# Gated linear attention: products of constants on TensorE at four kinds of waits

## What is computed

```python
def _gla_chunked(q, k, v, logg, s0):            # chunks of c = 64 tokens, 4 heads, dk = 32, dv = 64
    b = jnp.cumsum(logg.reshape(bsz, n, c, h, dk), axis=2)
    b_last = b[:, :, -1:]
    qe = q * jnp.exp(b)
    ke = k * jnp.exp(-b)
    att = jnp.where(causal, jnp.einsum('bnihd,bnjhd->bnhij', qe, ke), 0.0)
    o_intra = jnp.einsum('bnhij,bnjhv->bnihv', att, v)
    u = jnp.einsum('bnjhd,bnjhv->bnhdv', k * jnp.exp(b_last - b), v)
    decay = jnp.exp(b_last[:, :, 0])
    def step(state, xs):
        dec, uc = xs
        return dec[..., None] * state + uc, state
    s_fin, s_prev = lax.scan(step, s0, (decay by chunk, u by chunk))
    o_inter = jnp.einsum('bnihd,nbhdv->bnihv', qe, s_prev)
    return o_intra + o_inter, s_fin

def _gla_mixer(gq, gk, gv, glow, gr, s0, w_gate, b_gate, norm_g):
    logg = log_sigmoid(glow @ w_gate + b_gate) / 16
    o, s_fin = _gla_chunked(q / sqrt(32), k, v, logg, s0)
    return rmsnorm(o, norm_g) * silu(gr), s_fin
```

## Time and profile before

| | |
|---|---|
| median of 3 runs | 3492.03 us |
| the profiled execution's own time | 3492.51 us |
| its span, first to last instruction | 3490.8 us |
| PE busy | 3169.1 us, 91% of the span |
| DVE busy | 1812.2 us, 52% |
| ACT busy | 909.2 us, 26% |
| mean granted PE clock | 0.937 of full speed |

### The profile page before, as it was taken

How to read it: one execution, slowest core, us unless ns; L and a number is a source line. 1 busy time by engine, 2 the same in 40 slices (tenths; PEclk the granted TensorE clock), 3 DMA queues, 4 the chain that set the end, 5 groups by cost and what they waited for, 6 DMA issues and landing times. The chain is left out here.

```text
span 3490.8 us, 50998 instructions
## 1 busy us (share of the span) xinstructions
PE 3169.1 (91%) x20834; PEld 2795.9 (80%) x20834; DVE 1812.2 (52%) x3100; ACT 909.2 (26%) x1461; POOL 244.5 (7%) x280
## 2 busy tenths in 40 slices
PE   5986899799989999999979588998988999999998
PEld 5963477555889999999979455765568999999998
DVE  3853477444345454454556545774442554545445
ACT  3013344344231111111220224443442311111112
POOL 2000000242000000000020000003400000000000
PEclk9985799899999999999989758998999999999999
DMA  4111101364121111111021201015621211111111
GB/s 96 43 36 32 38 5 37 121 196 134 49 57 49 49 47 36 54 54 37 21 45 38 54 10 35 5 37 184 208 95 27 61 55 36 49 50 45 36 43 66
DMA packets 226512, 207.04 MB, mean 59 GB/s; under 512 B 50244, under 2 KB 195780, under 8 KB 226132
## 3 DMA queue, kind: packets, MB, share of 16 engines
q1 hardware_dynamic: 200728, 119.38, 12.7%
q0 software_dynamic: 25600, 85.11, 8.0%
HBM read 193.58 MB, written 11.05 MB: 59 GB/s over the span
## 5 line engine op out<-in xcount | busy, mean ns | idle before, releaser
L189 PE MATMUL ps<-streamH,upH 128*128 128x344 f32 x2112 | 449.9, 321 | 3.4 <-DVE upL L2291 3.4
L189 PE MATMUL ps<-streamH,upL 128*128 128x344 f32 x2112 | 448.4, 321 | 0.0
L189 PE MATMUL ps<-streamL,upH 128*128 128x344 f32 x2112 | 447.2, 320 | 0.0
L189 PEld LDWEIGHTS ps<-streamH,upH 128*128 128x128 f32 x2112 | 356.0, 188 | 4.1 <-DVE upL L2291 3.7
L189 PEld LDWEIGHTS ps<-streamH,upL 128*128 128x128 f32 x2112 | 357.0, 189 | 0.0
L189 PEld LDWEIGHTS ps<-streamL,upH 128*128 128x128 f32 x2112 | 353.9, 188 | 0.0
L2229 ACT ACTIVATE upH<-hc 128x1024 fp32r<-128x1024 f32 x88 | 93.5, 1063 | 975.4 <-PE ps L189 972.9
L2351 DVE TENSOR_TENSOR xT<-xT,ps 128x1032 f32<-128x1032 f32 x176 | 216.1, 1229 | 227.5 <-PE ps L189 227.5
L415 PE MATMUL ps<-inH,inW 128*128 128x344 f32 (+1 forms) x1248 | 237.4, 326 | 41.4 <-DVE inW L467 41.4
L2312 DVE TENSOR_TENSOR hc<-ps,rstd 128x1032 f32<-128x1032 f32 x44 | 54.3, 1233 | 371.4 <-PE ps L189 371.4
L415 PEld LDWEIGHTS ps<-inH,inW 128*128 128x128 f32 (+1 forms) x1248 | 201.4, 185 | 49.0 <-DVE inW L467 42.8
(11 more groups left out here) (461 smaller groups left out, 5093.0 us busy)
## 6 DMA issues: line engine op xcount, KB each, us to landing
hc<-in_w_ffn_in SPq DMA_DIRECT2D x88, 512.0 KB, 3.8
hc<-in_w_ffn_out SPq DMA_DIRECT2D x44, 512.0 KB, 3.7
big<-in_w_in SPq DMA_DIRECT2D x22, 512.0 KB, 3.9
stream_raw<-in_w_out SPq DMA_DIRECT2D x16, 512.0 KB, 4.0
big<-in_x_prompt SPq DMA_DIRECT2D x1, 4096.0 KB
out_y_prompt<-big SPq DMA_DIRECT2D x8, 512.0 KB
scratch_y<-hc SPq DMA_DIRECT2D x16, 136.0 KB
scratch_u<-wring SPq DMA_DIRECT2D x4, 516.0 KB
```

The costliest lines, as they stand in the source:

```text
L189: last = pe.matmul(self.ps[:, bank + n, 0:NCOL], w, x[:, n * NCOL:(n + 1) * NCOL], start=(k == 0 and i == 0), stop=(k == len(terms) - 1 an ...
```

## The change

A helper `keep_busy` multiplies the identity by the constant of ones, 128x128 by 128 columns, n times into a PSUM bank; the result is never read. Each bank used (0 in the preparation, 4 and 5 in the loop) is overwritten by the next product that goes there. PE runs 10 of them behind the waits for `c_zero` and `c_min` and ahead of the wait for `c_tre` 1, 16 ahead of the wait for `c_pre` 4, 6 ahead of the wait for `c_pre` 5 and `c_tre` 7, and 5 in each `second(n)` ahead of its waits for the mask and the state. The wait for `c_oc`, which guards the bank, moves to the front of `second`.

```diff
+    def keep_busy(self, pe, bank, n):
+        for _ in range(n):
+            pe.matmul(self.ps[:, bank, 0:P], self.C("ident", P), self.C("ones"), start=True, stop=True)
...
                 pe.wait_ge(c_zero, 1)
                 pe.wait_ge(c_min, 1)
+                self.keep_busy(pe, 0, 10)
                 pe.wait_ge(c_tre, 1)
                 for bank in (2, 3):
                     pe.matmul(ps[:, bank, :], S[0][:, 0:P], C("chunk_reset")[:, 0:512], start=True, stop=True)
+                self.keep_busy(pe, 0, 16)
                 pe.wait_ge(c_pre, 4)
                 pe.wait_ge(c_tre, 3)
...
                     last.then_inc(c_tr, 1)
+                self.keep_busy(pe, 0, 6)
                 pe.wait_ge(c_pre, 5)
                 pe.wait_ge(c_tre, 7)
...
                 def second(n):
+                    if n >= 2:
+                        pe.wait_ge(c_oc, n - 1)
+                    self.keep_busy(pe, 4 + n % 2, 5)
                     pe.wait_ge(c_attm, n + 1)
                     pe.wait_ge(c_st, 2 * n + 2)
-                    if n >= 2:
-                        pe.wait_ge(c_oc, n - 1)
```

## The result

The change takes 3523.2 us (median of 5 runs, 3510.2 to 3532.2) against 3490.5 for the kernel before (5 runs, 3486.6 to 3492.2): ratio 1.0092, interval 1.0063 to 1.0120. It is slower, by 33 us, where the forecast was no change at 3493.3 and the range ended at 3511.

What follows compares the result with a forecast made beforehand. TensorE was taken to bound GLA's loop, at 1.2 GHz and hardly ever waiting. Gains and losses summed to +0.4 us a layer, +0.8 in all: 3493.3 us, no change, range 3476 to 3511.

Steps and rivals of the forecast that it cites:

- Which level the loop has: GLA loop's clock: four of the first seven blocks at 2.4 GHz, the other four blocks at 1.2; decides the sign.
- fast block: A GLA loop block at 2.4 GHz: 5.55 us with its group, 2.1 less than before (bounds 1.4 to 2.6).
- Falling: Clock expected to fall behind first(0) and near sample()'s wait, from one row with 0.36 us of work in 4.8.
- Rising: Loop block's 3.3 us of dense work lies between 1.9 and 5.9 us, so the clock rises in some blocks only.
- rival 1: GLA loop stays mostly at 2.4 GHz: six fast blocks a layer 3476 us, all fast 3461; chance 0.28.
- Rival 2: Groups in second lift the clock too seldom, 2.3 us a block: 3511 us, or 3525 with none fast; chance 0.29.
- the preparation: GLA ahead of its loop: groups almost covered by waits, clock rising 1.9 to 5.9 us after 299.47, net gain 0.4 us.
- first(0) at 2.4 GHz: The first ahead of the loop runs at the higher clock, heads of 0.63 us, 1.8 us less a layer.
- the slow block: A GLA loop block at 1.2 GHz: nothing hides the group, so 7.67 + 2.3 = 10.0 us.
- its group: Five constant products in second, with the change of operand shape: 2.3 us at 1.2 GHz, 1.25 at 2.4.
- sample()'s wait: Ahead of first(6), if the loop is fast there: PE waits 2.3 us for DVE, once a layer.
- No transfer is added: In the GLA loop, the added products were taken to bring no further transfers; no cost was counted for any.

Runs made afterwards that it cites:

- e4: The change plus 8 more products behind first(0) and 8 more ahead of first(6): median 3490.5 us, ratio 1.0002 against the kernel before.
- e10: e6 with the products behind first(0), in first and ahead of first(6) contracting 64 rows instead of 128: 3526.3 us, ratio 1.0112 against the kernel before.
- e2: The change without the three groups of the preparation, the five products in each second kept: 3508.4 us, ratio 1.0044 against the kernel before.
- e5: The change with second's groups replaced by four products in mid-first, eight behind first(0), ten ahead of first(6): 3471.3 us, ratio 0.9953 against the kernel before.
- e6: e5 with 46 small products more in the first stage, making 512 more code records on PE than before: 3460.9 us, ratio 0.9919.
- e1: The change without the five products in each second, the preparation's three groups kept: 3494.9 us, ratio 1.0012 against the kernel before.
- e9: e6 with the products behind first(0), in first and ahead of first(6) contracting 32 rows instead of 128: 3514.7 us, ratio 1.0078 against the kernel before.
- e3: The kernel before with 72 one-row, one-column products at the end of the first stage, 288 more code records: 3503.2 us, ratio 1.0030.
- e12: The kernel before with 56 small products at the end of the first stage, 224 more code records on PE: 3515.3 us, ratio 1.0082.

## Why the prediction was wrong

**What failed is the step "Which level the loop has".** It counted four fast blocks in the first seven, and there was none in the profiled execution. Two readings in it were wrong. *Falling*: I had one row, a clock that fell while PE had next to no work, and took idleness for the cause. e4 shows it falling at 339.9 and 346.7, in a first, right behind 3.40 busy us of 3.40 and 3.20 of 3.20; e10 shows it falling behind 3.30 of 3.30. So a fast block loses the clock again by its own first. *Rising*: I set the 3.3 us of dense work in a block between 1.9 us at L1049 and 5.9 at L177, as if its length alone decided. The 1.9 was misread: between L1049 and the last first stand second(6) and second(7), so PE had run products of 128 rows for 8.7 us, from the row below, when the clock came up at 380.1.

```profile
371.39 1.12 PE L1024 MATMUL ps<-wring,big 128*64 128x256 f32 x4
```

The group stands between two firsts. In e2 and e4 the clock did rise some 3.2 us into such a group and its second (338.9, 343.3), in the change in none of the first seven blocks. I had seen the main thing, that busy PE with thin products stayed at 0.50, used it against rival 1, and didn't turn it on the fast block itself, which has 2.6 us of them.

**Rival 2 came, at its far end**: none fast behind first(0), 3525 forecast, 3523.2 measured. That closeness is partly luck. Its +16.2 a layer met +15.1; but 9 us of the total are the code's, which no case had, and the profiled execution of the change is its longest, 3532.2 us at a mean clock of 0.938; three others took 9 to 22 us less at 0.941 to 0.944, so they seem to have had some fast blocks. Which block rises differs from one execution to the next (e2's 94.5 us instead of 106 belongs here too). What decides it, I can't show.

**What held, term by term** (layer 1): the preparation, first(0) beginning 15.7 us into the stage instead of 16.1 (-0.4, as forecast), lifted at 302.8, inside the bounds; first(0) at 2.4 GHz with heads of 0.65 us (forecast 0.63, -1.7); the slow block 10.1 us (10.0), its group 2.43 (2.3); the sum -0.4 - 1.7 + 7 x 2.43 + 2.3 for the last group, less 1.9 for what ran faster behind it (L1035, L1045, L1057), is +15.3 against +15.1. The fast block, not seen in the change, was 5.7 us in e4 (forecast 5.55). sample()'s wait shows in e5, where ten products of 2.4 us and 0.28 more stand in it: 2.7 us against a forecast of 2.3.

**What was missing: code is work for PE too.** "No transfer is added" was wrong: 57 instruction packets are. In straight code the trace shows some 256 records of PE between two packets. Over three passes of the feed-forward loop, of about 1760 PE records each, the DMA queues (packets, MB, share) of the kernel before, from 1160 to 1580 us, have one row, and none of instructions; those of the change, from 1166 to 1592, have such a row:

```profile
q1 hardware_dynamic: 26707, 18.89, 15.3%
```

```profile
q8 instruction: 28, 0.46, 0.4%
```

So before, the loop's code stays with PE; in the change each pass fetches nine packets. Shown is that a shift by 256 or 512 records costs at most 1.7 us a layer and fetches no packet in the loop, and that six other shifts cost 2 to 12 us a layer; so the position within a packet decides, not the length. That the loop stays only where it touches seven packets and not eight (1760 / 256 = 6.9, which some seven positions in eight miss) fits all nine positions but is argued, not shown.

The Trainium skill, page "Runtime: NRT & Kernel Launch", section "Instruction fetch mechanics", says that TensorE holds 2048 instructions, fetched in blocks of 256 in sequence, and that a taken branch outside what is held waits for a fetch. The trace agrees, with 0.86 us of waiting at the edge shown above; with its sentence that only two blocks are held the loop of the kernel before does not, which ran without a packet from 1158 to 1584 us, 426 us.

The Trainium skill's page "TensorE: Matmul & The Clock Gate", section "Loop structure matters more than you think", calls matmuls back to back the good loop. By that e10 is as good as e6; the trace disagrees, 77.80 busy us of 77.80 at 0.50.

## What to carry to other kernels

In this kernel filling waits kept TensorE's clock only where the filling was of full height, stood inside the stretch of thin products and left no bare wait behind first(0): look at what a fall follows, and put products there too, not only where the idle time is. Here that turned +0.92% into -0.47% (e5), and with code padded to whole packets into -0.81% (e6), with 82 products a layer against the change's 72. And before costing instructions by their time alone, look at the instruction packets and the pauses marked "issue" at loop edges: in this kernel six of the eight lengths of code added to PE ahead of the feed-forward loop cost 7 to 20 us in its two stages, the two of whole packets next to nothing. That can make a good edit look like none (e1: 3 us gained in GLA, 0.1% slower).

## What I had not expected of the hardware

The clock fell under a TensorE that was busy all the time, where its filling was 64 rows high instead of 128 (e10; 32 in e9). Products that run once, in a wait of the first stage, cost 8.8 us in the feed-forward stages, the first of which begins a millisecond later (e3), and 20 us with 16 of them fewer (e12).
